# Merge gates by seven half-size products in blocks 1 to 7, in a gated two-mixer trunk on one core

## The chip, the cores and the metric

One core of one Trainium2 chip runs the whole kernel. The metric is the device time of one execution in microseconds (us). The engines are TensorE (PE, its weight loads shown as PEld), VectorE (DVE), ScalarE (ACT), GpSimd (POOL) and SyncE (SP, which here only issues DMAs).

## The reference

The input x has 4096 frames of 1024 channels. In float32, the part that is computed:

```python
h = rms_norm(x, norm_w) * (1 + scale) + shift      # scale, shift, gate from c
p = h @ w_in                                       # gq gk gv gz lr hq hf hi hz mg
o_g = rms_norm(chunk_gated_state(gq, gk, gv, log_a)) * silu(gz)
o_h = rms_norm(chunk_gated_state(silu(hq), 1 - f, hi, log_f)) * silu(hz)
g_a, g_b = split(sigmoid(mg + merge_b))            # mg: 2048 columns of p
m = g_a * (o_g @ w_up_gla) + g_b * (o_h @ w_up_hgrn)
out = rms_norm(x + gate * (m @ w_out), final_norm_w)
```

The change concerns mg, the merge gates: h (4096 x 1024) times 2048 columns of w_in. At the kernel's accuracy each matrix product is three passes on TensorE: every float32 operand is split into a high part (fp32r) and a low part, and hi*hi, hi*lo and lo*hi are summed.

## The kernel before

The frames run in 8 blocks of 512 (T), numbered 0 to 7. A block is 66 **slots**; a slot is one tile of weights, 128 x 1024 floats (512 KB), and the matmuls that use it. All five engines walk the same list of slots, each through its own loop `for s in range(SLOTS)`, and meet at semaphores; what an engine does in its round for slot s is called step s here. Nearly every step of ACT and DVE first waits for `slot_done` of its slot.

The slots of a block: 0 to 27 are the projections hf, gk and lr, hi, gv, gq, hq, gz and hz. Slots 28 to 51 hold the merge gates and up-projections in turn. A merge-gate slot (j, g) is `feature_major`: 8 slices of weights x 3 passes = 24 matmuls 128*128 by 128x512 into bank F[g]; ACT then writes sigmoid(F[g] + bias) to `gates`. Up-projection j is 24 such matmuls into two banks of A; DVE multiplies the banks by the two gates, adds them to `m_raw[:, j, :]` (this gives `up_used`), ACT copies it to m_hi and DVE subtracts to m_lo (`m_split`). Slots 52 to 65 (OUT0 on) are the output projection. It already goes by seven half-size products (Winograd's form of Strassen's method) in place of eight: 14 slots of 12 matmuls, which need sums of quarters of m. `m_sums` makes these on POOL as soon as m_split has come for both tiles of a pair, four adds of 128x256 in a chain; the last pair's are on DVE. `root_diagonals` (DVE, step 47) and `root_rows` (TensorE, slot 48) prepare the norm of the next block, `x_scale`, `h_high` and `h_low` its h.

Weights come in two ways. Raw: SP loads a slot to one of 4 `w_raw` buffers (`load_w`), four such loads ahead; at step s ACT copies the high part of slot s+3 to `w_hi` (`split_hi`) and DVE subtracts the low part to `w_lo` (`split_lo`); these are a ring of three slots. In block 0 all slots are raw, and SP stores both halves to DRAM (`keep_halves`; the ring place is free for the next split when the store has landed). In blocks 1 to 7, slots 3 to 51 come as halves: SP waits for slot_done of s and loads two tiles for s+3 (`load_halves`), with no work on ACT and DVE. Slots 0 to 2 and the output slots stay raw.

POOL in block 0: `out_pieces` loads the tiles of w_out, scales them by the gate and stores 14 tiles of combinations, in two rounds (q = 0, 1) over four buffers w_b. These lie where `o_tm` is written from step 21 on, so ACT waits for all 14 stores before it writes o_tm's first tile. The loads of x for the next block and their squares are in steps 37 to 44.

## Time and profile before

| | |
|---|---|
| time, median of 3 runs | 2838.88 us (2838.64 to 2839.45) |
| the profiled execution | 2838.43 us |
| its span, first to last instruction | 2836.6 us |
| TensorE busy | 2797.2 us, 99% |
| DVE / ACT / POOL busy | 1258.9 / 1023.2 / 297.1 us |
| granted TensorE clock, mean | 0.995 |
| DMA | 604.43 MB, 213 GB/s |

Times within the trace count from the first instruction. Busy times overlap between engines. For TensorE the busy time says little of how full it is, because the ends of pipelined matmuls are modelled and overlap the next one's start; the distance between two starts is the better measure. "Idle before" names what ended a wait. A block takes some 346.6 us.

### The profile page before, as it was taken

How to read it: one execution, taken by the hardware profiler on the slowest of the kernel's cores; microseconds unless marked ns; L12 is line 12 of the kernel's file. 1: busy time of each engine (PE TensorE's matmuls, PEld its weight loads, DVE VectorE, ACT ScalarE, POOL GpSimd, SP SyncE). 2: the span in 40 equal slices, each digit the busy share in tenths (PEclk: the TensorE clock that was granted, in tenths of full speed). 3: DMA queues.
4: the chain of work that ended last, by engine and by line, in shares of the span. 5: the costliest groups of instructions: out<-in, count | busy, mean ns of one | idle time of the engine just before them, and what ended most of it. 6: DMA issues, size and time to landing. Idle time of an engine off the chain costs nothing.

```text
span 2836.6 us, 35194 instructions
## 1 busy us (share of the span) xinstructions
PE 2797.2 (99%) x14328; PEld 2296.2 (81%) x14328; DVE 1258.9 (44%) x1779; ACT 1023.2 (36%) x1420; POOL 297.1 (10%) x415
## 2 busy tenths in 40 slices
PE   7999999999999999999999999999999999999998
PEld 4878888888887888878888888888888888888886
DVE  7765373432634235342453515525164251633416
ACT  3633345222452134521345213442134421443213
POOL 1441100111001010010100110001100011000101
PEclk9999999999999999999999999999999999999999
DMA  9987865455754557545575466654666546665454
GB/s 372 345 326 248 318 236 205 164 180 206 261 180 164 192 197 261 187 152 205 208 249 179 149 220 216 227 180 148 223 221 227 178 152 221 220 224 178 149 193 163
DMA packets 164129, 604.43 MB, mean 213 GB/s; under 512 B 18496, under 2 KB 18752, under 8 KB 162432
## 3 DMA queue, kind: packets, MB, share of 16 engines
q1 hardware_dynamic: 160544, 590.45, 59.5%
q0 software_dynamic: 3168, 11.54, 1.0%
q8 instruction: 114, 1.87, 0.3%
q14 instruction: 47, 0.39, 0.0%
q10 hardware_dynamic: 256, 0.20, 0.0%
HBM read 526.28 MB, written 75.63 MB: 212 GB/s over the span
## 4 chain that ended last, share of the span: by engine, by line
PE 97%; DVE 1%; DMA 1%; issue 0%; ACT 0%; SPq 0%; POOL 0%; POOLq 0%; DVEq 0%; ACTq 0%
PE F L1278 33%; PE A L1267 32%; PE A L1332 12%; PE A L1354 9%; PE F L1267 3%; PE F L1354 2%; PE R L1384 1%; PE F L1411 1%; PE A L1426 1%; PE F L1405 1%; DMA ada_w<-in_ada 1%; PE R L1377 1%; DVE h_tmp L873 0%; DVE gates L1030 0%; PE R L1216 0%
## 5 line engine op out<-in xcount | busy, mean ns | idle before, releaser
L1278 PE MATMUL F<-h_hi,w_hi 128*128 128x512 f32 x1408 | 553.9, 393 | 0.0
L1278 PE MATMUL F<-h_lo,w_hi 128*128 128x512 f32 x1408 | 548.2, 389 | 0.0
L1278 PE MATMUL F<-h_hi,w_lo 128*128 128x512 f32 x1408 | 548.2, 389 | 0.0
L1267 PE MATMUL A<-w_hi,h_hi 128*128 128x512 f32 (+1 forms) x1408 | 532.8, 378 | 0.0
L1267 PE MATMUL A<-w_lo,h_hi 128*128 128x512 f32 (+1 forms) x1408 | 523.2, 372 | 0.0
L1267 PE MATMUL A<-w_hi,h_lo 128*128 128x512 f32 (+1 forms) x1408 | 523.0, 371 | 0.0
L1030 DVE TENSOR_TENSOR gates<-gates,A 128x512 f32<-128x512 f32 x128 | 82.3, 684 | 543.5 <-PE A L1332 543.5
L866 DVE TENSOR_TENSOR w_lo<-w_raw,w_hi 128x1024 fp32r<-128x1024 f32 x185 | 242.4, 1311 | 160.8 <-ACT w_hi L619 160.3
L1278 PEld LDWEIGHTS F<-h_hi,w_hi 128*128 128x128 f32 x1408 | 264.3, 188 | 56.3 <-issue 1.7
L1267 PEld LDWEIGHTS A<-w_hi,h_hi 128*128 128x128 f32 x1408 | 264.5, 188 | 55.7 <-issue 8.8
L1278 PEld LDWEIGHTS F<-h_hi,w_lo 128*128 128x128 f32 x1408 | 264.3, 188 | 55.5
L1278 PEld LDWEIGHTS F<-h_lo,w_hi 128*128 128x128 f32 x1408 | 264.4, 188 | 55.1 <-issue 1.7
L1267 PEld LDWEIGHTS A<-w_hi,h_lo 128*128 128x128 f32 x1408 | 264.5, 188 | 46.8
L1267 PEld LDWEIGHTS A<-w_lo,h_hi 128*128 128x128 f32 x1408 | 264.8, 188 | 42.6 <-issue 0.2
L619 ACT ACTIVATE w_hi<-w_raw 128x1024 fp32r<-128x1024 f32 x185 | 195.6, 1057 | 203.9 <-PE A L1354 84.9
L733 ACT ACTIVATE gates<-F,col 128x512 f32<-128x512 f32 x128 | 88.1, 688 | 488.7 <-PE F L1278 488.7
L1332 PE MATMUL A<-o_hi,w_hi 128*128 128x512 f32 x512 | 199.2, 389 | 0.0
L1332 PE MATMUL A<-o_lo,w_hi 128*128 128x512 f32 x512 | 199.2, 389 | 0.0
L1332 PE MATMUL A<-o_hi,w_lo 128*128 128x512 f32 x512 | 199.2, 389 | 0.0
L499 POOL TENSOR_TENSOR rstd<-ssq,eps_t 128x4 f32<-128x4 f32 x64 | 34.0, 532 | 1145.6 <-DVE ssq L1158 1145.6
L741 ACT ACTIVATE m_hi<-m_raw 128x512 fp32r<-128x512 f32 x64 | 40.5, 633 | 290.9 <-DVE m_raw L1034 290.9
L1332 PEld LDWEIGHTS A<-o_hi,w_hi 128*128 128x128 f32 x512 | 96.1, 188 | 20.0
(214 smaller groups left out, 3557.9 us busy)
## 6 DMA issues: line engine op xcount, KB each, us to landing
w_hi<-halves SPq DMA_DIRECT2D x329, 512.0 KB, 3.6
w_lo<-halves SPq DMA_DIRECT2D x329, 512.0 KB, 4.5
w_raw<-pieces SPq DMA_DIRECT2D x112, 512.0 KB, 4.9
w_raw<-in_w_stream SPq DMA_DIRECT2D x71, 512.0 KB, 5.3
halves<-w_hi SPq DMA_DIRECT2D x47, 512.0 KB, 3.3
halves<-w_lo SPq DMA_DIRECT2D x47, 512.0 KB, 4.5
xy<-in_x SPq DMA_DIRECT2D x32, 512.0 KB, 6.2
result<-xy SPq DMA_DIRECT2D x32, 512.0 KB, 7.9
```

Of the source, the lines that this page charges most:

```text
L499: nc.gpsimd.tensor_tensor(dst, src, eps_t[:, 0:k], ALU.add).then_inc(pool_pow, 1)
L619: AF(w_hi[:, s % RING, 0:n], w_raw[:, r, 0:n], ACT.Copy).then_inc(w_hi_done, 1)
L733: AF(gates[:, j % 2, g, :], F[g][:, :], ACT.Sigmoid, bias=merge_b[:, g * KT + FEAT[j]:g * KT + FEAT[j] + 1]).then_inc(mg_used.sem, 1)
L741: AF(m_hi[:, j, :], m_raw[:, j, :], ACT.Copy).then_inc(m_hi_done.sem, 1)
L866: V.tensor_tensor(w_lo[:, s % RING, 0:n], w_raw[:, u % RAW, 0:n], w_hi[:, s % RING, 0:n].bitcast(fp32), ALU.subtract).then_inc(w_split, 1)
L1030: ins = V.tensor_tensor(gates[:, j % 2, g, :], gates[:, j % 2, g, :], A[2 * (j % 2) + g][:, :], ALU.mult)
L1267: last = mm(banks[t][:, 0:width], src[ia][:, k, t * P:(t + 1) * P], w_[iw][:, s % RING, kk * width:(kk + 1) * width], start=(k == 0 and n ...
L1278: last = mm(dst[:, :], w_[iw][:, s % RING, k * P:(k + 1) * P], h_[ia][:, k, :], start=(k == 0 and n == 0), stop=(k == KT - 1 and n == 2))
L1332: last = mm(A[2 * (j % 2) + g][:, :], w_[iw][:, s % RING, kk * P:(kk + 1) * P], o_[ia][:, kk, :], start=(k == 0 and n == 0), stop=(k == HE ...
L1354: last = mm(OUT_BANK[pair_][tt][:, :], src[ia][:, 2 * (2 * q + kk) + f, at:at + P], w_[iw][:, s % RING, kk * 512:(kk + 1) * 512], start=(f ...
L1377: last = mm(R[c][r * CHUNK:(r + 1) * CHUNK, g * P:(g + 1) * P], gk[fr, t, h * CHUNK:(h + 1) * CHUNK], v_g[fr, t, h * P:(h + 1) * P], start ...
L1384: last = mm(R[c][:, g * P:(g + 1) * P], kdec_h[fr, t, g * P:(g + 1) * P], v_h[fr, t, g * P:(g + 1) * P], start=True, stop=True)
```

## The change

In blocks 1 to 7 the gates of tiles (2, 3), (4, 5) and (6, 7) are computed pair by pair, as 2x2 block products by the same seven-product scheme: halves of the contraction (channels 0 to 511 and 512 to 1023), halves of the frames (256 early, 256 late), and the two tiles. One slot (`merge_seven`) is one product for both g: 2 x 4 slices x 3 passes = 24 matmuls of 128x256. Tiles 0 and 1 stay as they were, and so does block 0, in which the slots that aren't needed are empty. A block from 1 on has 75 slots in this order: 28 to 31 direct gates; 32, 33 up-projections 0 and 1; 34 to 40 seven products; 41, 42 up; 43 to 49 seven; 50, 51 up; 52 to 58 seven; 59, 60 up; 61 to 74 output.

What goes with it:
- `merge_pieces` on POOL in block 0 (after slot 28) stores 12 combinations of gate weights. `m_sums`, and POOL's norm steps for block 1, come behind it there. Its buffers lie in m_hi and m_lo, so ACT waits for its stores before it writes m_hi of tile 4 (step 50).
- `h_sums` on DVE and copies on ACT make four combinations of quarters of h (S1 to S4), steps 30 to 36.
- `merge_out` (ACT copies of banks to gates, 2 of 128x256 after four of the products; the four sigmoids after the last) and `merge_adds` (DVE adds of banks to gates, 8 a pair) collect the seven products.
- In blocks 1 to 7 the first two products' weights are halves; the other five are raw and split on ACT and DVE, and so are the weights of up-projections 2, 4 and 6.
- `out_stored`, x loads and squares for the next block go to steps 5 and 8 to 11 in blocks 1 to 6; load_pair comes at 55 and 58; root_diagonals at step 54, root_rows at slot 55.
- ACT and SP wait for out_pieces buffer by buffer, and POOL's second round too; m_hi and m_lo of tile 5 are made with those of tile 6.

The core of the diff:

```diff
+PAIR_AT = [28, 34, 43, 52]
+UP_SLOT = {32: 0, 33: 1, 41: 2, 42: 3, 50: 4, 51: 5, 59: 6, 60: 7}
+UP_SPLIT = {s: (5, 6) if j == 6 else (j,) for s, j in UP_SLOT.items() if j != 5}
-XR_AT = 48
+XR_AT = 55
+T_OF = {2: 0, 3: 1, 4: 2, 6: 3}
 def from_raw(b, s):
-    return b == 0 or s not in KEPT
+    if b == 0:
+        return not empty(b, s)
+    return s not in KEPT or s in (41, 50, 59) or (s in SEVEN and SEVEN[s][1] in (*T_OF, 5))
...
+            def merge_pieces():
+                G = nc.gpsimd.tensor_tensor
+                pool.wait_ge(slot_done, DONE[0, 28])
+                for p in range(1, 4):
+                    for i, (to, f) in enumerate(((0, 0), (3, 0), (0, 1), (3, 1))):
+                        if p > 1:
+                            pool.wait_ge(m_b_out[i], 16 * (p - 1))
+                        at = PAIR_AT[p] + to
+                        pool.dma_start(m_b[i][:, :, :], w_stream[at:at + 3:2, :, 512 * f:512 * f + 512]
+                                       .rearrange("g p n -> p g n")).then_inc(m_b_in[i], 16)
+                    for n, (to, x0, x1, piece) in enumerate(((0, 1, 0, 1), (1, 3, 1, 3), (3, 3, 0, 2), (2, 2, 3, 0))):
...
+                        G(m_b[to][:, :, :], m_b[x0][:, :, :], m_b[x1][:, :, :], ALU.subtract).then_inc(m_b_link, 1)
...
+            def merge_out(b, p, n):
+                if n == 1:
+                    act.wait_ge(up_used.sem, up_used.at(b, 2 * p))
+                for at, (j, late, y) in {1: (ja, 0, 1), 2: (ja, 1, 2), 3: (jb, 1, 1), 4: (jb, 0, 0)}.items():
+                    if n == at:
+                        for g in range(2):
+                            last = AF(gates[:, j, g, halves_[late]], mg_banks(p, g)[y][:, 0:256], ACT.Copy)
+                        last.then_inc(m_cp.sem, 1)
...
+                    for i, at in ((S1, 33), (S2, 34), (S4, 35), (S3, 35)):
+                        if b and s == at:
+                            act.wait_ge(hs.sem, hs.at(b, {S1: 5, S2: 7, S4: 8, S3: 6}[i]))
+                            AF(S_hi[i], S_raw[i], ACT.Copy).then_inc(hs_hi.sem, 1)
+                    for j in UP_SPLIT.get(s, ()):
                         act.wait_ge(up_used.sem, up_used.at(b, j + 1))
+                        if b == 0 and j == 4:
+                            for i in range(4):
+                                act.wait_ge(m_b_out[i], 48)
                         AF(m_hi[:, j, :], m_raw[:, j, :], ACT.Copy).then_inc(m_hi_done.sem, 1)
...
                             if i == 0:
                                 act.wait_ge(out_stored.sem, out_stored.at(b, 0))
-                                act.wait_ge(pieces_out, PIECES * 16)
+                            if b == 0 and i < 4:
+                                act.wait_ge(pieces_out[i], 16 * (2 if i == 1 else 4))
+                                act.wait_ge(pieces_link, 16 if i == 3 else 15)
...
+            def merge_adds(b, p, n):
+                for at, after, j, late, y in ((1, 1, 0, 0, 0), (5, 4, 1, 0, 1), (6, 4, 0, 1, 0), (6, 4, 1, 1, 0)):
+                    if n == at:
+                        dve.wait_ge(m_cp.sem, m_cp.at(b, c0 + after))
+                        for g in range(2):
+                            part = gates[:, j, g, 256 * late:256 * late + 256]
+                            last = V.tensor_tensor(part, part, mg_banks(p, g)[y][:, 0:256], ALU.add)
+                        last.then_inc(m_add.sem, 1)
+            def h_sums(b, s):
+                TT = V.tensor_tensor
+                if s in (30, 31):
+                    for i, f, late in ((S2, 0, 0), (S3, 0, 1)) if s == 30 else ((S1, 1, 1), (S4, 1, 0)):
+                        TT(S_raw[i], h_quarter(h_hi, f, late).bitcast(fp32), h_quarter(h_lo, f, late).bitcast(fp32),
+                           ALU.add).then_inc(hs.sem, 1)
+                for at, n, to, x0, x1, op in ((32, 4, S1, S1, S3, ALU.add), (32, 5, S3, S2, S3, ALU.subtract),
+                                              (33, 6, S2, S1, S2, ALU.subtract), (33, 7, S4, S4, S2, ALU.subtract)):
...
+                for n, (i, at) in enumerate(((S1, 34), (S2, 35), (S4, 36), (S3, 36))):
+                    if s == at:
+                        dve.wait_ge(hs_hi.sem, hs_hi.at(b, n + 1))
+                        TT(S_lo[i], S_raw[i], S_hi[i].bitcast(fp32), ALU.subtract).then_inc(hs_lo.sem, 1)
...
+            def merge_seven(b, s, p, n):
+                if n == 0:
+                    if p == 1:
+                        pe.wait_ge(mg_used.sem, mg_used.at(b, 4))
+                    else:
+                        pe.wait_ge(m_add.sem, m_add.at(b, c0))
+                if n == 2:
+                    pe.wait_ge(up_used.sem, up_used.at(b, 2 * p - 1))
+                if n == 4:
+                    pe.wait_ge(m_add.sem, m_add.at(b, c0 + 1))
+                if n in (3, 5, 6):
+                    pe.wait_ge(m_cp.sem, m_cp.at(b, c0 + {3: 1, 5: 3, 6: 4}[n]))
+                of_h = {0: (0, 0), 1: (1, 0), 2: (1, 1)}
+                of_s = {3: S1, 4: S2, 5: S4, 6: S3}
+                if n in of_s:
+                    pe.wait_ge(hs_lo.sem, hs_lo.at(b, of_s[n] + 1))
...
+                for g in range(2):
+                    if p == 3 and n == 0 and g == 1:
+                        pe.wait_ge(up_used.sem, up_used.at(b, 6))
```

`mg_banks(p, g)` gives F0, F1, A0 for g = 0, and for g = 1 R0, R1, A1 in the first two groups and A2, A3, A1 in the third.

## Rows read from the trace of the kernel before

**Rows 1.** The page's part 1: busy us, share of span, instructions.
```profile
PE 2797.2 (99%) x14328; PEld 2296.2 (81%) x14328; DVE 1258.9 (44%) x1779; ACT 1023.2 (36%) x1420; POOL 297.1 (10%) x415
```
**Rows 2.** Waits of PE: engine, line, releaser: us, times, longest.
```profile
PE F L1405 <- issue: 6.0, 1, 6.0
```
**Rows 3.** Timeline of PE: start us, us, engine, line, op, out<-in, shapes.
```profile
1109.67 0.39 PE L1267 MATMUL F<-w_hi,h_hi 128*128 128x512 f32 x1
...
1115.11 0.28 PE L1267 MATMUL A<-w_hi,h_hi 128*128 128x272 f32 x1
...
1127.21 0.40 PE L1267 MATMUL A<-w_hi,h_hi 128*128 128x512 f32 x1
...
1189.97 0.28 PE L1458 MATMUL R<-la_hi,tri 128*128 128x256 f32 x1
...
1190.91 0.40 PE L1278 MATMUL F<-h_hi,w_hi 128*128 128x512 f32 x1
```
**Rows 4.** Timelines of PE and DVE in block 3, around up-projection 0.
```profile
1297.11 0.39 PE L1278 MATMUL F<-h_hi,w_hi 128*128 128x512 f32 x1
...
1297.37 1.29 DVE L1030 TENSOR_TENSOR gates<-gates,A 128x512 f32<-128x512 f32 x2 [9.04 <-PE A L1332]
1298.69 0.69 DVE L1034 TENSOR_TENSOR m_raw<-gates 128x512 f32<-128x512 f32 x1
1300.14 0.69 DVE L1047 TENSOR_TENSOR m_lo<-m_raw,m_hi 128x512 fp32r<-128x512 f32 x1 [0.76 <-ACT m_hi L741]
```
**Rows 5.** Timeline of DVE: two operations of 128x1024 in a row.
```profile
1408.69 2.35 DVE L1067 TENSOR_TENSOR s_lo<-m_raw,s_hi 128x1024 fp32r<-128x1024 f32 x2
```
**Rows 6.** Two lines of ACT: ns min/median/max, first and last start us, forms.
```profile
L619 ACT ACTIVATE w_hi<-w_raw x185: 1039/1061/1116, 36.1 to 2817.0; 128x1024 fp32r<-128x1024 f32 x183, 128x1088 fp32r<-128x1088 f32 x2
...
L811 ACT ACTIVATE o_tm<-F x64: 367/378/394, 184.5 to 2627.3; 128x256 f32<-128x256 f32 x64
```
**Rows 7.** Timelines of DVE and POOL: root_diagonals alone and beside m_sums; out_pieces.
```profile
28.05 0.87 DVE L873 TENSOR_SCALAR h_tmp<-ident,x_rs 128x128 f32<-128x128 f32 x4
...
1382.46 1.86 DVE L873 TENSOR_SCALAR h_tmp<-ident,x_rs 128x128 f32<-128x128 f32 x4
...
1382.62 0.74 POOL L567 TENSOR_TENSOR m_raw<-m_raw 128x256 f32<-128x256 f32 x1 [14.96 <-DVE m_lo L1047]
...
100.43 2.42 POOL L534 TENSOR_TENSOR w_b<-w_b,gate_bc 128x1024 f32<-128x1024 f32 x1
```
**Rows 8.** Timelines of DVE and PE in block 3, output slot 4.
```profile
1410.96 1.22 DVE L866 TENSOR_TENSOR w_lo<-w_raw,w_hi 128x1024 fp32r<-128x1024 f32 x1
...
1412.60 0.39 PE L1354 MATMUL F<-w_hi,m_hi 128*128 128x512 f32 x1
```
**Rows 9.** Timelines of POOL and ACT in block 0, around the end of out_pieces.
```profile
174.95 0.58 POOL L528 DMA_DIRECT2D pieces<-w_b  x1 [0.30 <-POOL w_b L556]
...
184.49 0.66 ACT L811 ACTIVATE o_tm<-F 128x256 f32<-128x256 f32 x2 [10.92 <-DMA pieces<-w_b]
```
**Rows 10.** DMA issues (page; last one 80 to 176 us); windows ending in DMA share, GB/s.
```profile
w_lo<-halves SPq DMA_DIRECT2D x329, 512.0 KB, 4.5
...
pieces<-w_b POOLq DMA_DIRECT2D x14, 512.0 KB, 8.0
w_b<-in_w_stream POOLq DMA_DIRECT2D x8, 512.0 KB, 10.4
...
halves<-w_lo SPq DMA_DIRECT2D x16, 512.0 KB, 8.3
...
120.00:140.00 20.00, 19.97 (x87) 15.82 (x86) 17.24 (x11) 15.30 (x20) 8.54 (x8) 1.00 1.02 392
...
260.00:280.00 20.00, 20.00 (x89) 16.54 (x89) 7.45 (x9) 5.89 (x9) 2.15 (x3) 1.00 0.84 306
```
**Rows 11.** Timelines of DVE and PE in block 3: lf_lo and who needs it.
```profile
1169.74 2.29 DVE L1093 TENSOR_TENSOR lf_lo<-z_f,lf_hi 128x2048 fp32r<-128x2048 f32 x1 [5.17 <-ACT lf_hi L768]
...
1177.22 0.39 PE L1450 MATMUL R<-lf_hi,tri 128*128 128x512 f32 x1
```

More of the change, by code:

```diff
@@ L423, in body @@
                             if USES[u + RAW] == (0, OUT0):
-                                sp.wait_ge(pieces_out, PIECES * 16)
+                                pieces_kept(sp)
+                            if USES[u + RAW] == (1, PAIR_AT[1] + 2):
+                                for i in range(4):
+                                    sp.wait_ge(m_b_out[i], 48)
                             load_w(u + RAW)
-                    if not first and s + RING in KEPT:
+                    if not first and s + RING in KEPT and not from_raw(b, s + RING):
@@ L433, in body @@
-                    if s + early in (37, 38) and not last:
-                        load_x(b + 1, s + early - 37)
-                    if s + early == 43 and not last:
-                        for t in (2, 3):
-                            sp.wait_ge(x_sq.sem, x_sq.at(b + 1, t - 1))
-                            load_x(b + 1, t)
-                    if s + early in (50, 51) and not last:
-                        sp.wait_ge(x_sq.sem, x_sq.at(b + 1, s + early - 47))
-                        load_pair(b + 1, s + early - 50)
@@ L442, in body @@
-                    if s in (54, 65) and not last:
-                        n = 1 if s == 54 else 2
+                    if first:
+                        if s in (39, 41):
+                            load_x(1, s // 41)
+                        if s == 48:
+                            for t in (2, 3):
+                                sp.wait_ge(x_sq.sem, x_sq.at(1, t - 1))
+                                load_x(1, t)
+                        if s in (59, 60):
+                            sp.wait_ge(x_sq.sem, x_sq.at(1, s - 56))
+                            load_pair(1, s - 59)
+                    elif not last:
+                        if s == 5:
+                            sp.wait_ge(out_stored.sem, out_stored.at(b, 0))
+                            for t in range(NT):
+                                sp.dma_start(x_first[:, t, :], x[bass.ds((b + 1) * T + t * P, P), :]).then_inc(
+                                    first_x_in[t], 16)
+                        if s in (55, 58):
+                            sp.wait_ge(x_sq.sem, x_sq.at(b + 1, 4))
+                            sp.wait_ge(slot_done, DONE[b, s])
+                            load_pair(b + 1, s // 58)
@@ L444, in body @@
+                    if s in (63, 74) and not last:
+                        n = 1 if s == 63 else 2
                         sp.wait_ge(h_split.sem, h_split.at(b + 1, n))
                         load_pair(b + 1, n + 1)
-                    if s in (54, 56):
-                        if s == 54:
+                    if s in (63, 65):
+                        if s == 63:
                             sp.wait_ge(up_used.sem, up_used.at(b, 8))
-                        for t in (0, 1) if s == 54 else (2, 3):
-                            if s == 56:
+                        for t in (0, 1) if s == 63 else (2, 3):
+                            if s == 65:
@@ L518, in out_pieces @@
                 G = nc.gpsimd.tensor_tensor
-                steps, stored = [0], [0]
+                steps, stored = [0], [0] * 4
                 def done(ins):
@@ L548, in out_pieces @@
                     gated(1, q)
-                    pool.wait_ge(pieces_out, 16 * stored[0])
+                    for i in (0, 2, 3):
+                        pool.wait_ge(pieces_out[i], 16 * stored[i])
                     done(G(w_b[:, 0, :], w_b[:, 1, :], w_b[:, 0, :], ALU.subtract))
@@ L580, in body @@
                     out_pieces()
+                elif not last:
+                    for t in range(NT):
+                        x_tile(b + 1, t)
                 for i in range(8):
@@ L584, in body @@
                     inverse_root(rstd[:, fam, 4 * t:4 * t + 4], ssq[:, fam, 4 * t:4 * t + 4], rstd_ready)
+                if first:
+                    merge_pieces()
                 m_sums(b, 0)
                 m_sums(b, 1)
-                if not last:
+                if first:
                     for t in range(NT):
```

194 lines of the change are left out of this document (143 added, 51 removed).

## The prediction, made before the changed kernel was run

> **What bounds the kernel now.** I read the page's first part before anything else: TensorE is busy 99% of the span, the next engine 44% [rows 1]. The list of waits by engine, cut to TensorE, has one wait after the start that is longer than a microsecond: 6.0 us before an output product in block 0 [rows 2]. So TensorE's issue rate is the bound, and the time of a change is its matmul stream plus whatever holds that stream. "Busy" can't price a matmul, because the modelled ends overlap (0.39 us each). I take the distance between starts instead: 24 matmuls of 512 columns take 1115.11 - 1109.67 = 5.44 us, 0.2267 each; 96 of 272 columns take 12.10 us, 0.1260 each; 8 of 256 columns take 0.94 us, 0.1175 each [rows 3]. Nothing stands between slots: a slot of 24 wide matmuls is 5.44 us.
>
> **The matmul stream.** In blocks 1 to 7 each of three pairs of merge-gate tiles goes from 4 slots x 24 matmuls of 512 columns (96 x 0.2267 = 21.76 us) to 7 slots x 24 of 256 columns (168 x 0.1175 = 19.74 us). That is 2.02 us a pair, and 21 pairs give **-42.4 us**. The other end: a line through the 272 and 512 rows gives 0.1193 at 256, 1.72 us a pair, -36 us. I take 0.1175, the row of exactly this width. The new slot is 2.82 us long, and this is the point: everything that ACT and DVE do per slot must now fit in about half the time.
>
> The Trainium skill ("TensorE: Matmul & The Clock Gate", Back-to-back issue gap, and LDWEIGHTS) says that the spacing is set by the weight load too, and prices a load of 128 columns at 107 ns, by which the half-size product would sit just at the edge. The rows at 256 columns show 0.1175 with a weight load before each, so it would change the sum by nothing; loads exposed in full are a rival below.
>
> **First pair: DVE's queue.** The new sums of four quarters of h are 8 adds and 4 subtracts of 128x1024 on DVE and 4 copies on ACT in each block from 1 on; they stand in steps 30 to 36 and TensorE needs them from the fourth product (slot 37). Prices for this size: DVE 1.22 us [rows 8], and 2.35 for two in a row, so 1.13 to the next [rows 5]; ACT 1.06 [rows 6]. An add of 128x256 with a PSUM operand I put at 0.35, an estimate from two of 128x512 in 1.29 [rows 4]. I lay block 3 of the trace out anew. Slot 33 (second up-projection) would end its issue at 1297.11 + 5.44 = 1302.55 [rows 4]; DVE sees a slot's end 0.26 later (1297.11 against 1297.37) and needs 2.0 us from there to m_raw [rows 4]. DVE after slot 32: gate products and m_raw to 1299.4, m_lo to 1300.8 [rows 4], two sums to 1303.2. After slot 33: gate products and m_raw to 1305.15, split of slot 36's weights 1306.3, m_lo 1306.9, sums 1308.0 and 1309.3, split for slot 37 1310.4, first low half of a sum 1311.6. TensorE wants slot 37 at 1302.55 + 3 x 2.82 = 1311.0: 0.6 us late. One slot later split, two adds and a low half take 3.0 us against 2.82: 0.2 more. That makes 0.8 us a block without disturbance.
> There is one. m_sums on POOL (4 adds, 0.74 each) starts when m_lo of tile 1 is ready, at 1306.9, in the middle of this queue. In the trace the four tensor_scalars of root_diagonals take 0.87 us alone and 1.86 beside the first two of such POOL adds [rows 7]: each POOL add holds DVE by 0.5 us. Four of them fall before the second low half: 4 x 0.54 = 2.1. So the hold is 2.9 us a block, 7 blocks, **+20.3 us**. Ends: 0.8 (5.6) and, with the whole 0.74 each, 3.7 (26).
> The Trainium skill ("SBUF — State Buffer", SBUF: two separate sides) has the lock of the port pair held for the whole instruction of whoever came first, for DVE operations with two SBUF inputs. By it the hold would be 3.7 and the sum 2836; the rows show 0.5 of the 0.74.
> Second pair, laid out the same way: no sums, POOL's adds meet only the splits; slot 46 needs its split 2.7 us after it is there. No hold. ACT per half slot: split 1.06 and two copies 0.7 (0.37 each [rows 6]) = 1.8 of 2.82; the adds feed products two slots on. No hold.
>
> **Third pair.** Its first product's second half goes to A2 and A3, which up-projection 5, the slot just before, fills; it waits for m_raw of tile 5, 0.26 + 2.0 + 0.06 = 2.3 us after the slot's end, and the first half covers 1.41. Queued behind it: all of TensorE. 0.9 x 7 = **+6.3 us**. Ends 0.6 and 1.2.
> root_diagonals moves to step 54 and TensorE's root_rows to the end of slot 55, one half slot later: after seeing the slot's end, ACT split 1.06, DVE split 1.2, diagonals 0.87 make 3.4 + 0.06 against 2.82, **+3.6 us** over the 6 blocks that have a next one; ends 0 and 8.
>
> **Into the output products.** Splits for output slot 4 end at 1410.96 + 1.22 = 1412.2, and TensorE begins that slot at 1412.60 [rows 8]: 0.4 us of slack, the least in this part. New ahead of it: ACT's last four sigmoids wait for the last adds and finish 5.6 us into slot 59, so h_high, the next split and DVE's behind it come 0.3 later; DVE has m_lo of tile 5 as well (0.6); and m_sums of tiles 4 and 5 now starts here, two of its adds between DVE's h_low operations (1.1). Less DVE's idle time of 0.4 there, 1.5 us of lag against 0.4 of slack: 1.1 x 6 (block 7 has no h_low) = **+6.6 us**, ends 0 and 12.
>
> **Block 0.** Gain: the output product that waits 6.0 us waited for ACT, ACT (10.92 us) for the landing of the last of 14 stores, issued at 174.95 [rows 9]. Now each tile waits for its own buffer: the first one's last store is issued some 10 us earlier, before ACT gets there at 173.6. **-6.0 us**; what is late next is nothing, since DVE and ACT have slots of 5.44 there.
> Cost: merge_pieces on POOL, 12 loads, 12 subtractions of 2.42 us [rows 7] and 12 stores between slot 28 and the wait of ACT at step 50, behind which m_hi and the split for slot 54 are queued; TensorE feels it when ACT is later than about 100 us after slot 28. A round is 0.5 + load + 3 x (2.4 + 0.9) + store; with 10.4 and 8.0 [rows 10] 28.8 us, the first one 31.6 with its fourth subtraction: 89 us, in time by 11. But the DMA engines are at 0.84 in this stretch at 306 GB/s, so full at 364; another 12.6 MB in 90 us is 140 GB/s more, 446, where the fullest window shows 392 [rows 10]. Stores of halves then land in 8.3 us [rows 10], and the ring of three now turns over every second slot (10.88 us) where it had three slots: 8.3 + 1.06 + 1.2 + POOL's share is 11 to 12 us. I take **+4 us**, ends 0 and 28 (below).
>
> **Moved at no cost.** The x loads and squares for the next block go to steps 5 and 8 to 11. ACT gets four squares there, at some 1.3 us each (estimated from its 1.06 for this size), beside the exp and ln work; at most three of them, 3.9 us, push lf_lo, which ends at 1172.0 for a TensorE step that begins at 1177.22 [rows 11]. With that cover of 5.2 us gone, each us more would be 6 in all. SP's new wait for the stored results at step 5 comes 16 us after their issue and holds nothing. Loading slots 36 to 41 (and 45 to 50, 54 to 59) raw moves DMA bytes from 2 x 512 KB to 512 KB and costs the splits counted above. The halves for slots 42, 44, 51, 53 and 60 have 8.3 us to land instead of 10.9; the median landing of the slower of the two is 4.5 [rows 10], which hides them.
>
> **Sum**, against the profiled execution's 2838.43 us (span 2836.6 and 1.8 around it; the median of the three runs is 2838.88, so the same within 0.5): 2838.4 - 42.4 + 20.3 + 6.3 + 3.6 + 6.6 - 6.0 + 4 = **2831 us**.
>
> **Rivals.**
> A: DVE's queue is shorter than I lay it out (POOL's adds fall in its gaps, TensorE buffers the rest). For it: DVE is busy 44% only. Against: the rows 7. First pair 5.6, third 6.3 and 2, output 0, block 0 nothing: 2838.4 - 48.4 + 13.9 = 2804 us.
> B, on the other side: block 0 fills up. If a load and a store on POOL's queue together take 30 us instead of 18.4, a round is 40 us, three end 125 us after slot 28, ACT is some 25 us over what TensorE tolerates: 2831 - 4 + 28 = 2855. It decides from a sum of 25 us on. For it: 446 GB/s asked where 392 were shown. Against: in the stretch of 120 to 140 us the same queues shared with output pieces, and TensorE did not stop.
> C: the second and third pairs are held like the first (halves or splits late): + 14 x 2.9 = 2871. The layout speaks against it.
> D: a 256-column matmul can't cover its weight load of 0.188 busy: 168 x 0.188 = 31.6 us a pair, + 21 x 11.9 = 3081 us. The 272 rows, with the same loads at 0.126, rule it nearly out.
> E: the change does not do what it says, TensorE's matmuls of 512 columns stay: 2832 to 2836, only block 0's terms. The diff leaves no path for this from block 1 on.
>
> **Chances.** Forecast 0.45 (own range 2820 to 2843), A 0.26, B 0.19, C 0.07, D 0.02, E 0.01. A measurement of this kernel can tell about 0.2% (5.7 us) from no change: faster is below 2833, slower above 2845. Faster: A and somewhat over half of the forecast, 0.51; slower: B but for a bit, C and D, 0.28; the same 0.21. The range 2802 to 2858 leaves out C, D and the far ends of A and B.
>
> **What would show it.** Right: 3528 matmuls of 128x256 at 0.1175; in each block from 1 on a stop of 2 us before slot 37 and 0.7 before slot 38, released by DVE's low halves; a stop of 0.9 in the middle of slot 52; no 6.0 us wait in block 0. Wrong: no stop at slot 37 (A); ACT idle before an m_hi in block 0, released by a POOL store (B); stops in slots 43 to 49 (C). What would make the number wrong most easily is the length of DVE's queue in steps 32 to 35: 1 us there is 7 us in all.

## The result and the profile after

The changed kernel takes **2853.2 us** (median of 6 runs, 2847.5 to 2855.5) where the kernel before takes 2838.6 (6 runs on the same chip): ratio 1.0051, 95% interval 1.0039 to 1.0063. That is slower, by 0.5%. 2831 was predicted, a small gain. The time fell inside the range given (2802 to 2858), on the other side of no change and outside the forecast's own part of it (2820 to 2843). The profiled execution took 2851.9 us, with a span of 2850.1.

From its page: the line that answers to [rows 1], the chain that ended last (shares of the span by engine), and one of the costliest groups of instructions (us in total, mean ns of one, then idle time before them):

```profile
PE 2781.8 (98%) x15840; PEld 2349.2 (82%) x15840; DVE 1588.8 (56%) x2157; ACT 1220.4 (43%) x1742; POOL 410.2 (14%) x451
...
PE 86%; DVE 8%; issue 2%; ACT 2%; DMA 1%; SPq 0%; POOL 0%; POOLq 0%; ACTq 0%; DVEq 0%
...
L681 POOL TENSOR_TENSOR m_raw<-m_raw 128x256 f32<-128x256 f32 x24 | 28.2, 1176 | 819.7 <-DVE m_lo L1223 819.7
```

TensorE is still 98% busy, but DVE is now 8% of the chain that ended last (1% in the kernel before), and one of POOL's small adds takes 1176 ns on average where 0.74 us stood in [rows 7]. The list of TensorE's waits (engine, tile, line, releaser: us in total, times, longest us) has six lines that before's did not have (the first six here; the seventh stood there once, with 0.2), and the 6.0 us of [rows 2] are gone:

```profile
PE F L1490 <- DVE S_lo L1176: 14.0, 10, 2.1
PE F L1459 <- DVE w_lo L1014: 5.0, 1, 5.0
PE A L1490 <- DVE m_raw L1210: 4.7, 7, 0.7
...
PE A L1573 <- DVE w_lo L1014: 3.1, 7, 0.5
PE R L1596 <- DVE a_cols L1307: 3.0, 1, 3.0
PE F L1573 <- DVE w_lo L1014: 2.6, 7, 0.4
PE R L1397 <- DVE h_tmp L1021: 2.3, 6, 0.4
```

Waits alone don't add up to a difference, so I cut TensorE's timeline of both kernels at the first matmul of each stretch and compare the lengths. In blocks 1 to 7 each stretch has the same length to 0.03 us, but for the first group of three pairs (last column of the second row):

| stretch | before, us | after, us | difference over the run |
|---|---|---|---|
| three groups of products, if nothing holds them | 21.76 each | 20.15 each | 21 x -1.60 = -33.6 |
| first group, above 20.15 | 0 | 2.61 in three blocks, 3.51 in three, 3.80 in one | +22.2 |
| third group, above 20.15, block 7 (without root_rows) | 0 | 0.92 | 7 x 0.92 = +6.4 |
| root_rows in the third group, blocks 1 to 6 | 1.22 | 1.51 | 6 x 0.29 = +1.8 |
| output products, blocks 0 to 6 | 38.21 | 39.77 to 39.90 | +11.6 |
| block 0 up to the output products | 362.03 | 366.28 | +4.3 |
| up-projections, and block 7's output products | | | +1.1 |
| sum | | | +13.8 |

2838.4 + 13.8 = 2852.2, against 2851.9 measured. So next to nothing is missing, and each row can be set against a term of the prediction.

**The matmul itself.** The second group of block 3, which nothing holds, from its first matmul to the first of the slot behind it:

```profile
1344.45 0.28 PE L1490 MATMUL F<-h_hi,w_hi 128*128 128x256 f32 x1
1344.56 0.28 PE L1490 MATMUL F<-h_lo,w_hi 128*128 128x256 f32 x1
1344.68 0.28 PE L1490 MATMUL F<-h_hi,w_lo 128*128 128x256 f32 x1
...
1364.60 0.40 PE L1551 MATMUL A<-o_hi,w_hi 128*128 128x512 f32 x1
```

168 matmuls in 20.15 us are 0.1199 each. The first distance of the stretch is 0.11 and all others are 0.12. The 0.1175 of [rows 3] came from eight matmuls of another kind (la_hi and la_lo with tri, into R). All eight stand 0.117 to 0.119 apart; why they are closer than those of the products is not shown.

**The first group.** DVE (five rows) and POOL (the first of four adds that follow one another) in block 3 while the first three products run, then TensorE (start us, us, and in brackets the idle time before and its releaser):

```profile
1314.07 1.22 DVE L1172 TENSOR_TENSOR S_raw<-S_raw 128x1024 f32<-128x1024 f32 x1
1315.32 1.65 DVE L1172 TENSOR_TENSOR m_units<-m_units,S_raw 128x1024 f32<-128x1024 f32 x1
1316.90 1.76 DVE L1014 TENSOR_TENSOR w_lo<-w_raw,w_hi 128x1024 fp32r<-128x1024 f32 x1
1318.58 1.74 DVE L1176 TENSOR_TENSOR S_lo<-S_raw,m_unitsr 128x1024 fp32r<-128x1024 f32 x1
1320.25 1.75 DVE L1014 TENSOR_TENSOR w_lo<-w_raw,w_hi 128x1024 fp32r<-128x1024 f32 x1
...
1314.23 1.66 POOL L681 TENSOR_TENSOR m_raw<-m_raw 128x256 f32<-128x256 f32 x1 [30.94 <-DVE m_lo L1223]
...
1318.39 0.28 PE L1490 MATMUL A<-h_hi,w_lo 128*128 128x256 f32 x1
1320.47 0.36 PE L1490 MATMUL F<-m_unitsr,w_hi 128*128 128x256 f32 x1 [1.80 <-DVE S_lo L1176]
...
1321.35 0.41 PE L1490 MATMUL F<-m_unitsr,w_lo 128*128 128x256 f32 x1
1321.56 0.41 PE L1490 MATMUL F<-m_unitsr,w_hi 128*128 128x256 f32 x1
```

DVE goes from one operation to the next without idling, and each of the four that stand beside a POOL add takes 0.5 us more than the 1.22 before them. POOL's adds take twice their own 0.74. TensorE stops for 1.80 us before slot 37. Behind the stop its matmuls are 0.21 us apart. The granted clock says why (windows: us, busy of PE, PEld, DVE, ACT, POOL, granted clock, DMA share, GB/s; before the stop, behind it, and behind the same stop one block earlier):

```profile
1309.88:1318.50 8.62, 8.62 (x73) 8.58 (x71) 8.55 (x9) 6.78 (x9) 4.11 (x3) 1.00 0.17 61
1320.40:1324.00 3.60, 3.53 (x18) 3.56 (x19) 3.60 (x5) 0.85 (x3) 0.51 (x1) 0.56 0.55 173
...
973.18:976.50 3.32, 3.11 (x24) 2.91 (x24) 3.32 (x5) 0.96 (x4) 0.44 (x1) 1.00 0.50 175
```

In block 3 the granted clock fell from 2.4 to 1.2 GHz after the stop: 17 matmuls at 0.21 cost 1.55 us above the pitch (the distance between two starts). In block 2 an equal stop (1.80 us) left it at 1.00. There TensorE came to slot 38 early instead and waited again for DVE, so that the two cases differ by 0.9 us only:

```profile
973.18 0.36 PE L1490 MATMUL F<-m_unitsr,w_hi 128*128 128x256 f32 x1 [1.80 <-DVE S_lo L1176]
...
976.65 0.36 PE L1490 MATMUL F<-m_unitsr,w_hi 128*128 128x256 f32 x1 [0.36 <-DVE S_lo L1176]
```

**Block 0.** The stop of before (6.2 us between starts above the pitch, 6.0 of them idle), and the 0.7 of slow matmuls behind it, are gone. There are two new stops, of 3.0 and 5.0 us, with 1.5 of slow matmuls behind each. That makes -6.9 + 4.5 + 6.5 = +4.1 of the 4.3. This row is of one execution. Experiments 1, 2 and 3 leave block 0 as it is, and in their profiles it takes 360.12, 367.76 and 369.60 us up to the output products: the stop before a_cols is missing in the first and 3.2 and 3.9 long in the others, the one before slot 46 is 4.2, 4.3 and 7.0 long. The first stop, with what DVE and POOL did ahead of it:

```profile
158.61 2.40 POOL L643 TENSOR_TENSOR w_b<-w_b 128x1024 f32<-128x1024 f32 x1 [5.90 <-DMA pieces<-w_b]
...
162.01 4.48 DVE L1303 TENSOR_TENSOR kdec_h<-pk,row_bc 128x2048 f32<-128x2048 f32 x1
...
169.71 0.20 DVE L1307 COPY a_cols<-R 128x48 f32<-128x48 f32 x1
...
170.05 0.69 PE L1596 MATMUL R<-v_g,gk 64*64 64x128 f32 x16 [2.98 <-DVE a_cols L1307]
```

In the kernel before:

```profile
160.13 2.28 DVE L1124 TENSOR_TENSOR kdec_h<-pk,row_bc 128x2048 f32<-128x2048 f32 x1
161.72 2.95 POOL L550 TENSOR_TENSOR w_b<-w_b 128x1024 f32<-128x1024 f32 x1 [5.48 <-DMA pieces<-w_b]
```

The second, before slot 46: TensorE waits for DVE's split, DVE for ACT's, ACT 10.75 us for a store of halves:

```profile
301.55 1.06 ACT L738 ACTIVATE w_hi<-w_raw 128x1024 fp32r<-128x1024 f32 x1 [10.75 <-DMA halves<-w_lo]
302.64 1.22 DVE L1014 TENSOR_TENSOR w_lo<-w_raw,w_hi 128x1024 fp32r<-128x1024 f32 x1 [5.20 <-ACT w_hi L738]
...
303.92 0.79 PE L1459 MATMUL F<-h_hi,w_hi 128*128 128x512 f32 x1 [5.01 <-DVE w_lo L1014]
```

**Third group and output products** (block 3): slot 52's second half, root_rows, and the two stops of the output products that stand in the list of waits:

```profile
1377.77 0.38 PE L1490 MATMUL A<-h_hi,w_hi 128*128 128x256 f32 x1 [0.67 <-DVE m_raw L1210]
1388.49 1.12 PE L1397 MATMUL R<-h_tmp,one 128*128 128x512 f32 x2 [0.39 <-DVE h_tmp L1021]
1417.77 0.50 PE L1573 MATMUL A<-w_hi,m_hi 128*128 128x512 f32 x1 [0.46 <-DVE w_lo L1014]
1421.17 0.50 PE L1573 MATMUL F<-w_hi,m_hi 128*128 128x512 f32 x1 [0.39 <-DVE w_lo L1014]
```

### The profile page after: what moved, and what is told of

It is laid out like the page before. It is cut to its first block, busy times and chain, and to the rows that moved or that the text cites. A ratio compares the mean times of both kernels' runs of the same rounds, so it can differ in the third digit from the quotient of the medians.

```text
span 2850.1 us, 39215 instructions
## 1 busy us (share of the span) xinstructions
PE 2781.8 (98%) x15840; PEld 2349.2 (82%) x15840; DVE 1588.8 (56%) x2157; ACT 1220.4 (43%) x1742; POOL 410.2 (14%) x451
## 4 chain that ended last, share of the span: by engine, by line
PE 86%; DVE 8%; issue 2%; ACT 2%; DMA 1%; SPq 0%; POOL 0%; POOLq 0%; ACTq 0%; DVEq 0%
PE A L1448 31%; PE F L1459 18%; PE A L1551 8%; PE A L1573 7%; PE F L1490 5%; PE R L1490 3%; PE A L1490 3%; PE F L1448 3%; DVE w_lo L1014 2%; PE F L1573 2%; DVE gates L1206 1%; PE R L1603 1%; PE F L1630 1%; ACT w_hi L738 1%; PE A L1645 1%
## 5 line engine op out<-in xcount | busy, mean ns | idle before, releaser
L1014 DVE TENSOR_TENSOR w_lo<-w_raw,w_hi 128x1024 fp32r<-128x1024 f32 (+1 forms) x311 | 409.6, 1318 | 242.0 <-ACT w_hi L738 240.3
L738 ACT ACTIVATE w_hi<-w_raw 128x1024 fp32r<-128x1024 f32 (+1 forms) x311 | 328.5, 1057 | 432.7 <-PE A L1490 106.1
L1459 PE MATMUL F<-h_hi,w_hi 128*128 128x512 f32 x736 | 290.8, 395 | 5.0 <-DVE w_lo L1014 5.0
L1459 PE MATMUL F<-h_lo,w_hi 128*128 128x512 f32 x736 | 287.3, 390 | 0.0
L1459 PE MATMUL F<-h_hi,w_lo 128*128 128x512 f32 x736 | 287.2, 390 | 0.0
L1459 PEld LDWEIGHTS F<-h_hi,w_hi 128*128 128x128 f32 x736 | 138.6, 188 | 34.3 <-DVE w_lo L1014 5.4
L1459 PEld LDWEIGHTS F<-h_hi,w_lo 128*128 128x128 f32 x736 | 138.4, 188 | 29.2
L1459 PEld LDWEIGHTS F<-h_lo,w_hi 128*128 128x128 f32 x736 | 138.7, 188 | 28.0 <-issue 0.2
L681 POOL TENSOR_TENSOR m_raw<-m_raw 128x256 f32<-128x256 f32 x24 | 28.2, 1176 | 819.7 <-DVE m_lo L1223 819.7
L1324 DVE SCALAR_TENSOR_TENSOR S_h<-S_h,a_cols,R 128x128 f32<-128x128 f32 x256 | 71.8, 342 | 78.8 <-PE R L1603 77.7
L1551 PEld LDWEIGHTS A<-o_hi,w_lo 128*128 128x128 f32 x512 | 96.1, 188 | 20.2
```

Of the source, the lines that this page charges most:

```text
L738: AF(w_hi[:, s % RING, 0:n], w_raw[:, r, 0:n], ACT.Copy).then_inc(w_hi_done, 1)
L1014: V.tensor_tensor(w_lo[:, s % RING, 0:n], w_raw[:, u % RAW, 0:n], w_hi[:, s % RING, 0:n].bitcast(fp32), ALU.subtract).then_inc(w_split, 1)
L1324: ins = V.scalar_tensor_tensor(out=S_h[:, c, g, :], in0=S_h[:, 1 - c, g, :], scalar=a_cols[:, g, n:n + 1], in1=R[c][:, g * P:(g + 1) * P], ...
L1459: last = mm(dst[:, :], w_[iw][:, s % RING, k * P:(k + 1) * P], h_[ia][:, k, :], start=(k == 0 and n == 0), stop=(k == KT - 1 and n == 2))
L1551: last = mm(A[2 * (j % 2) + g][:, :], w_[iw][:, s % RING, kk * P:(kk + 1) * P], o_[ia][:, kk, :], start=(k == 0 and n == 0), stop=(k == HE ...
```

## Experiments

Each kernel is the changed one with the edit shown, unless said otherwise. Ratios are to the kernel before on the same chip (2838.1 to 2838.7 us). Differences are between medians, to the changed kernel's 2853.2.

**1. POOL's adds moved out of the first group** (x1_msums_late).

```
 c0: def m_sums(b, jp):
+                if b and jp == 0:
+                    pool.wait_ge(hs_lo.sem, hs_lo.at(b, 4))
```

> One wait added: in blocks 1 to 7 POOL's m_sums of the first pair waits until DVE has finished the last low half of the sums of h (step 36), so its four adds no longer stand between DVE's operations before slots 37 and 38. Theory 1 (DVE's queue of sums, drawn out by POOL's four adds by 0.5 us each, makes the stop before slot 37, and TensorE's clock falls in that stop): the four DVE operations that took 1.65 to 1.76 us are back at 1.22, the stop before slot 37 is at most 0.4 us, the 0.4 us before slot 38 is gone, the granted clock stays at 1.0 there, and the time falls by 7 x (1.8 to 2.4 of the stop + 1.5 of slow matmuls) = 23 to 27 us, to 2826 to 2830 us. Theory 2 (the queue is long by itself; POOL takes port time that would be waited for anyway): the stop stays at 1.5 us or more and the time is 2845 us or more. If a stop of 1 us or so stays but the clock does not fall, in between: 2833 to 2838.

Measured 2834.4 us (2828.0 to 2836.1), ratio 0.9985, interval 0.9976 to 0.9995; the profiled execution, the fastest of the ten, has a span of 2826.2. DVE's operations in the stretch are back at their own length, and the wait for S_lo is 2.3 us over the whole run in place of 14.0:

```profile
PE F L1492 <- DVE S_lo L1178: 2.3, 7, 0.6
...
1305.30 1.22 DVE L1174 TENSOR_TENSOR m_units<-m_units,S_raw 128x1024 f32<-128x1024 f32 x1
1306.44 1.22 DVE L1016 TENSOR_TENSOR w_lo<-w_raw,w_hi 128x1024 fp32r<-128x1024 f32 x1
1307.58 1.22 DVE L1178 TENSOR_TENSOR S_lo<-S_raw,m_unitsr 128x1024 fp32r<-128x1024 f32 x1
```

The first group is 0.61 us above 20.15 now (4.3 over the run, where it was 22.2). So 18 of the 22 us come from four POOL adds a block that nobody needed at that time. The rest, 0.6 a block, is DVE's queue without any disturbance; 0.8 was laid out. The granted clock stays at 1.00 behind the stops that are left (0.3 to 0.6 us idle).

The profile's span fell by 24 us and not by 18, because its block 0, which the edit doesn't touch, is 6.2 shorter than in the changed kernel's profile. POOL's second round of output pieces began there only as kdec_h was ending:

```profile
158.70 2.28 DVE L1305 TENSOR_TENSOR kdec_h<-pk,row_bc 128x2048 f32<-128x2048 f32 x1
...
160.88 2.39 POOL L643 TENSOR_TENSOR w_b<-w_b 128x1024 f32<-128x1024 f32 x1 [6.07 <-DMA pieces<-w_b]
```

**2. The sums of h one step earlier** (x2_sums_early): all steps 30 to 36 of the sums, except the last low half, become 29 to 35, on DVE and ACT.

```
-                if s in (30, 31):
+                if s in (29, 30):
-                for at, n, to, x0, x1, op in ((32, 4, ...), (32, 5, ...), (33, 6, ...), (33, 7, ...)):
+                for at, n, to, x0, x1, op in ((31, 4, ...), (31, 5, ...), (32, 6, ...), (32, 7, ...)):
-                for n, (i, at) in enumerate(((S1, 34), (S2, 35), (S4, 36), (S3, 36))):
+                for n, (i, at) in enumerate(((S1, 33), (S2, 34), (S4, 35), (S3, 36))):
```

> h_sums and their high halves one step earlier each (sums in steps 29 to 32, low halves in 33 to 36), POOL left as it is. Theory 1: DVE was idle in part of steps 29 to 31, so two operations of 1.22 us leave the queue after slot 33 and the low halves stand one slot earlier; no stop at slot 37 even beside POOL's adds, clock at 1.0, time down by 7 x 3.5 = 25 us to about 2828 us. Theory 2 (the stop only moves: DVE or ACT is now late for slots 34 to 36, whose splits wait behind the sums): stops of 1 to 2 us before slot 36 or 37, time 2840 to 2853 us.

Measured 2832.0 us (2829.0 to 2833.8), ratio 0.9976 (0.9966 to 0.9986). POOL's adds still lie beside DVE's queue, but the queue has a slot more to run in: the first group is 20.15 in all seven blocks, and there is no wait for S_lo in the list at all. The term is a matter of where the sums stand, not of their cost. This gain, 21.2, and the 18.8 of experiment 1 are less than the 25 and the 23 to 27 expected: that of experiment 1 counted 1.5 us a block of slow matmuls in full (see 8), and that of experiment 2 took 3.5 a block where the first group held 3.2.

**3. The stop kept busy** (x3_fill).

```
+                if p == 1 and n == 3:
+                    for i in range(15):
+                        mm(A[2][:, 0:256], w_hi[:, s % RING, (i % 8) * P:(i % 8 + 1) * P],
+                           h_quarter(h_hi, 1, 0)[:, 0, 0, :], start=True, stop=True)
```

> In the stop before slot 37 (blocks 1 to 7) TensorE does 15 matmuls of 128x256 (1.8 us) into bank A2, whose content nobody reads; all else as in the changed kernel. The computed result is unaffected. Theory 1 (the 17 matmuls at 0.21 us behind the stop are the price of the stop itself, which lets the clock fall to its lower level): slot 37 begins when it did, its matmuls are at 0.12 from the first on, the granted clock stays at 1.0, and the time falls by 7 x 1.5 = 10 us to about 2843 us. Rival (the clock falls there for another reason, such as the many short matmuls before it): 0.21 stays and the time stays at 2853 us or rises by what the added matmuls overrun.

Measured 2849.9 us (2843.0 to 2852.1), ratio 1.0036 (1.0023 to 1.0049): 3.3 us less, where about 10 had been expected from the slow matmuls. Block 0 varies by several us from one execution to the next, so I repeated the comparison with block 0 quiet (8, below).

**4. Block 0's ring by count of slots** (x6_ring3). A ring of three buffers serves slots by s % 3. In block 0 three of the seven slots of each group are empty, so that some buffers come up again after two slots of work. The edit deals the three buffers out to the slots that do hold work.

```
+def place(b, s):
+    return (DONE[0, s] - 1) % RING if b == 0 else s % RING
-                 AF(w_hi[:, s % RING, 0:n], w_raw[:, r, 0:n], ACT.Copy)
+                 AF(w_hi[:, place(b, s), 0:n], w_raw[:, r, 0:n], ACT.Copy)
```

> Block 0 only: the place in the ring of three for a slot's halves goes by the count of slots that are not empty, and the split looks three such slots ahead, as it did before the change; loads, stores and POOL's work are as in the changed kernel. Theory 1 (block 0's stop of 5.0 us before slot 46 comes from the ring that turns over every second slot: ACT waits 10.75 us for halves to be stored before it may split again): that stop and the slow matmuls behind it (1.5 us) are gone, ACT's waits for halves stores are under 3 us, time down by 5 to 7 us to about 2847 us. Rival (the DMA engines are full, whatever the ring): the stop stays within 2 us of its length or moves to a later slot, time 2851 to 2855 us.

Measured 2845.4 us (2843.2 to 2848.5), ratio 1.0024 (1.0014 to 1.0035), 7.9 us less than the changed kernel. The 5.0 us stop is gone from the list of waits. The stores are no faster: from 200 to 330 us the second store of a slot lands in 9.4 us (median), in the changed kernel in 7.0. ACT's waits for them are even longer in sum and up to 6.2 us long, where under 3 had been expected, but none is long enough for TensorE to feel it (ACT's waits: the changed kernel, then this one):

```profile
ACT w_hi L738 <- DMA halves<-w_lo: 22.2, 5, 10.8
```

```profile
ACT w_hi L756 <- DMA halves<-w_lo: 26.4, 10, 6.2
```

**5. A third of the new traffic** (x4_one_group).

```
-                for p in range(1, 4):
+                for p in range(1, 2):
```

(with the loads of all groups from the first group's five pieces)

> Leaves out: POOL makes the five pieces of weights of the first pair of merge-gate tiles only (4 loads, 4 subtractions, 4 stores in place of 12 of each), and the second and third pair use them again, so their outputs are not the reference's. The rest, the ring of block 0 too, is as in the changed kernel. Theory 1, the stop of 5.0 us before slot 46 of block 0 (and the 1.5 us of slow matmuls behind it) comes from the traffic of this work, which slows the stores of halves: the stop is gone, about -6 us, 2847. Rival, the ring of three alone makes it, by coming round every second slot: the stop stays, 2853.

Measured 2845.9 us (2839.7 to 2848.8), ratio 1.0025 (1.0014 to 1.0035). The stop is gone with the ring as it was, and so are nearly all of ACT's waits for stores of halves, which land in 4.0 us where they took 7.0:

```profile
ACT w_hi L738 <- DMA halves<-w_lo: 2.7, 1, 2.7
```

4 and 5 together: the stop needs both, the stores that merge_pieces' traffic slows and the ring that comes round every second slot. Taking away either one removes it.

**6. Tile 5's split of m two steps earlier** (x5_m5_at57).

```
-UP_SPLIT = {s: (5, 6) if j == 6 else (j,) for s, j in UP_SLOT.items() if j != 5}
+UP_SPLIT = {s: (j,) for s, j in UP_SLOT.items() if j != 5}
+UP_SPLIT[57] = (5,)
```

> Only the split of tile 5 of m moves, from step 59 to step 57, in all blocks. Theory 1: the stops in front of the output products (0.6 + 0.55 + 0.25 us a block over the pitch) come from DVE, which at steps 59 and 60 has this split more and is slowed by POOL's adds of tiles 4 and 5 that follow it; they shrink to 0.4 a block, -8 us in 8 blocks: 2845. Rival, they come from ACT (four sigmoids, h_high and the split of weights): no change, 2853.

Measured 2842.9 us (2837.6 to 2845.5), ratio 1.0016 (1.0007 to 1.0024): 10.3 less. In the profile 8.4 of this stand in the output products; the rest is within what block 0 varies. The output products of blocks 1 to 6 take 38.73 us each, where they took 39.88 (before: 38.21). POOL's adds of these tiles now start at 1395.58 and not at 1408.09, they take 0.74 each instead of 0.74 to 1.12, and the two h_low operations of DVE take 1.41 us together instead of 2.38 (the changed kernel, then this one):

```profile
1407.33 1.29 DVE L1223 TENSOR_TENSOR m_lo<-m_raw,m_hi 128x512 fp32r<-128x512 f32 x2
1408.54 2.38 DVE L1044 SCALAR_TENSOR_TENSOR h_lo<-xf,s_col,h_hi 128x512 fp32r<-128x512 f32 x2
```

```profile
1406.46 0.68 DVE L1224 TENSOR_TENSOR m_lo<-m_raw,m_hi 128x512 fp32r<-128x512 f32 x1
1407.07 1.41 DVE L1045 SCALAR_TENSOR_TENSOR h_lo<-xf,s_col,h_hi 128x512 fp32r<-128x512 f32 x2
```

DVE gets through this stretch 1.6 us earlier by that: 0.6 for the split and 1.0 for the overlap. 1.15 of it arrives at TensorE. Of the 0.5 a block that stays over before, 0.3 stands at output slot 4 and 0.2 at output slot 6.

**7. Edits 2, 4 and 6 together, and more** (x7_three; x8_four; x9_pool_wait_all).

```
 (x8)
+def up_bank(j):
+    return 2 * ((j + (j in (4, 5))) % 2)
-                 A[2 * (j % 2) + g][:, :]
+                 A[up_bank(j) + g][:, :]
 (x9)
+                    else:
+                        for i in range(4):
+                            pool.wait_ge(pieces_out[i], 16 * stored[i])
```

> Three edits together: sums of h one step earlier, tile 5's split at step 57, the ring of block 0 by count of slots. If the stops they remove are separate places on TensorE's path, they add: -21 (measured for the first), -7.9 (for the ring), -8 (expected for the split) from 2853: 2816. If the time of one only reappears at the next stop, 2825 or more.

> As x7_three, and up-projections 4 and 5 exchange their PSUM banks, so that the first product of the third pair finds its second bank free. Theory 1: the stop of 0.67 idle (0.9 over the pitch) in slot 52 of 7 blocks goes, -6 us from x7_three: 2810. Rival: TensorE is held later by that much (at root_rows or slot 54, which now needs tile 5's product): as x7_three, 2816.

> As x8_four, but before POOL's second round of output pieces it waits for all eight stores of the first, as the kernel before did, so that its four adds run about 3 us later and no longer beside DVE's kdec_h. Theory 1: the stop of 2.5 us at 166 us (TensorE waits for a_cols of DVE) and the 1.5 us of slow matmuls behind it go, -4 us: 2801. Rival, DVE is as late without the overlap, or ACT's wait for the stores, now later, holds the output product at 178 us: 2805 or more.

x7_three: 2812.9 us (2811.4 to 2814.1), ratio 0.9912 (0.9899 to 0.9926). The three gains measured alone, 21.2, 7.9 and 10.3, make 39.4, and 40.3 came. They are separate places on TensorE's path and add up: in the profile the first groups are at 20.15 and the output products at 38.74. x8_four: 2805.1 (2803.8 to 2807.4), ratio 0.9886 (0.9872 to 0.9899); the third group is 0.93 us shorter in all seven blocks, 6.5 in sum, and its wait for m_raw is gone. x9_pool_wait_all: 2803.9 (2802.9 to 2804.7), ratio 0.9877 (0.9864 to 0.9891). The times of these last two can't be told apart (1.3 us, where 4 had been expected), but the profiles differ: the span of x9 is 3.3 us shorter, TensorE's wait for a_cols, 2.5 us in x8_four, is gone, and DVE's kdec_h, with POOL's adds 5.4 us later, is done in 2.28 us (x8_four's wait; then x9's rows):

```profile
PE R L1621 <- DVE a_cols L1332: 2.5, 1, 2.5
```

```profile
160.81 2.28 DVE L1331 TENSOR_TENSOR kdec_h<-pk,row_bc 128x2048 f32<-128x2048 f32 x1
...
163.12 2.40 POOL L671 TENSOR_TENSOR w_b<-w_b 128x1024 f32<-128x1024 f32 x1 [5.05 <-DMA pieces<-w_b]
```

**8. What the lower clock costs** (x10_slow_sums, the changed kernel with edits 4 and 6; x11_slow_sums_fill, the same with the fill of experiment 3).

> The changed kernel with the ring of block 0 by count of slots and tile 5's split at step 57, while the sums of h stay where the changed kernel has them, so that the stop before slot 37 stays. By the runs so far 2853 - 8 - 8 to 10 = 2835 to 2837. It is the base for x11_slow_sums_fill.

> x10_slow_sums with 15 more matmuls of 128x256 on TensorE in the stop before slot 37 (1.8 us of work, results not used). Theory 1, a stop costs its length and about 1.5 us more, because TensorE comes back at the lower clock: without idling there the slow matmuls go, -1.5 x 7 = -10 us from x10_slow_sums: 2825 to 2827. Rival, the slow matmuls are time that TensorE would lose at the next wait for DVE in any case (slot 38): -3 us or less.

x10_slow_sums: 2834.7 us (2831.5 to 2837.2), ratio 0.9986 (0.9978 to 0.9995). x11_slow_sums_fill: 2832.6 (2829.0 to 2833.7), ratio 0.9976 (0.9966 to 0.9985). The spans are 2834.9 and 2831.5. So the fill is worth 2 to 3.4 us: the expectation of 10 was wrong, and its rival holds. The granted clock behind the stop of block 3, without the fill and with it:

```profile
1311.60:1315.20 3.60, 3.55 (x18) 3.58 (x19) 3.60 (x5) 0.84 (x3) 0.49 (x1) 0.57 0.55 181
```

```profile
1310.93:1314.53 3.60, 3.28 (x28) 3.11 (x27) 3.60 (x5) 1.17 (x4) 0.32 (x1) 1.00 0.54 187
```

The clock does stay up, and 28 matmuls fit where 18 did. But DVE, not TensorE, sets the time in this stretch: the matmuls that are now in time wait at slot 38 (0.3 us of idle time in each block). The first group is 22.8 long in six blocks with the fill and 23.1 in one; without it 23.7 in four, 22.8 in two and 23.1 in one. Four blocks times 0.9 are 3.6, and the spans differ by 3.4.

## Why the prediction was wrong, step by step

**Matmul stream**, -42.4 forecast, -33.6 measured, the largest error (8.8 us), and outside the other end of 36. The step that failed is the price of 0.1175 from eight matmuls [rows 3]. The steady distance is 0.1199, and 0.0024 x 3528 is 8.5 us. The eight are another kind of matmul and stand 0.117 to 0.119 apart throughout, so counting rows of the same width was not enough. The line through 272 and 512 gave 0.1193 and was nearer, though I took it for the less likely end. With both widths measured in long stretches, 256 columns more cost 0.2267 - 0.1199 = 0.1068 us, which leaves 0.0131 us in each matmul, wide or narrow. That fixed part eats into the gain: seven eighths of 21.76 us would be 19.04, a gain of 2.72 a group, and 1.60 came. Four slots of 24 wide matmuls hold 96 x 0.0131 = 1.3 us of it, seven of half width 2.2.
The Trainium skill ("TensorE: Matmul & The Clock Gate", Back-to-back issue gap) gives the gap of a single matmul at the higher clock as N / 2.4 + 2.5 ns. The trace agrees with the first term (106.8 ns for 256 columns) and not with the second: 13 ns at both widths.

**First pair**, +20.3 forecast, +22.2 measured: right in place (before slots 37 and 38) and cause. 0.5 us for each of POOL's four adds beside DVE is what the rows show, and experiment 1 separates the parts: 0.6 a block is queue (0.8 forecast), and where the clock stayed up 2.0 is POOL's (2.1 forecast). These two alone make 18.3 in seven blocks. The rest is what I did not see, that TensorE's clock may fall after the stop: 0.9 in each block where it does, four of seven here. So the named parts come out 2 us under the forecast, and the unnamed one puts the sum 2 us over it.
The Trainium skill ("SBUF — State Buffer", SBUF: two separate sides) would have the lock held for the whole instruction. Here DVE lost 0.43 to 0.54 us to each add of 0.74 us, as in [rows 7], and POOL lost more, its adds taking 1.59 to 1.66. With long operations the loss is nearly whole: kdec_h, begun 0.08 us after a POOL add of 2.42, took 4.48 in place of 2.28.

**Third pair and root_rows**, +6.3 and +3.6 forecast, +6.4 and +1.8 measured. The wait for m_raw in slot 52 is right to 0.1 us; experiment 7 removes it by another choice of banks. root_rows was mis-sized by 0.3 a block.

**Output products**, +6.6 forecast, +12.1 measured (+11.6 in blocks 0 to 6, and 0.5 in block 7). The mechanism is the one named, and experiment 6 shows it. Of the size, 1.66 a block against 1.1, 1.15 is tile 5's split with the POOL adds behind it; 0.5 stays when both are moved, and what that rests on is not settled (the forecast's 0.3 for the sigmoids is a candidate that no run tests). Block 0 has the cost too and was left out of the sum.

**Block 0**, -2 forecast, +4.3 measured up to the output products in this execution, and +5.7 and +7.6 in those of experiments 2 and 3. Two steps failed.
The gain of 6.0 us from separate waits was real at the place, but I said that nothing is late next. The same edit lets POOL begin its second round buffer by buffer, here at 158.61 instead of 161.72. Its second add falls on DVE's kdec_h, which then takes 4.48 us in place of 2.28. TensorE waits 3.0 us for the a_cols behind it, and 1.5 more go in slow matmuls. With x9's wait the overlap and the stop are gone, but one profile doesn't show that the wait is the reason: of the eleven other profiles from the changed kernel on, x1_msums_late and x7_three also have kdec_h alone (2.28), without any such edit. In x1 there is no stop before a_cols either, and block 0 comes out 1.9 us under before, as forecast; in x7 1.5 us remain, behind a split of DVE's that a POOL add drew out to 3.98. The other nine have kdec_h at 4.47 to 4.50 and stops of 1.5 to 3.9. So POOL beside DVE is the cause that fits every profile, and whether they meet is a race between executions.
The cost of the new traffic was put at 4, as a delay of stores of halves in a ring that turns over every second slot: that is what happened, once a run, and it cost 5.0 + 1.5 here. The slow matmuls behind the stop were missing from the price.

**The rivals.** A (2804) was wrong: DVE's queue is as long as laid out, although DVE is busy only 56%. B (2855) has nearly the measured time, but not by its mechanism: ACT was to be held at step 50 by merge_pieces' stores. It wasn't: no wait of ACT for those stores is in its list. What held ACT was the store of halves, which I had as a term of the forecast. The time lies outside the forecast's own range (2820 to 2843). It lies inside the whole range only because that takes in B, so that it is inside by luck. C and D are out: the second group stands at 20.15 in every block. E is out by 3528 matmuls of 128x256.

In sum, the failed steps are the pitch, the size of the output products' delay, and block 0's "what is late next is nothing": of the 21 us between forecast and profile 8.8 are the matmul's pitch, 6.3 block 0, 5.5 the output products and 1.9 the first group, less 1.8 at root_rows. Apart from the pitch, what was left out is of two kinds: an overlap of POOL and DVE at a place that I had not laid out (kdec_h, block 0's output products), and the clock after a stop.

## What to carry to other kernels

Take the pitch of a matmul from a long steady stretch of the same kind of matmul, and split it into a part that goes with the columns and a part that does not, before multiplying it by thousands: cutting matmuls in half doubles the second part. When a change shortens a slot, lay out the queue of the elementwise engine for it, with every POOL operation that will run beside it, and then look for a step where the same work would be hidden; here moving the sums of h by one step, one split by two steps, one pair of banks and one ring turned +0.5% into -1.1% (x8_four). An earlier start of an engine off the path isn't free: ask beside what it will now run.
